# Squares of group B's outputs two steps later, and their roots one step later, in the lead to forgetting attention

## The reference, cut to what matters

```python
u = rmsnorm(h, g_attn)
qa, ka, va, logf, qb, kb, vb = project(u, w_in, b_forget)
oa = fox_prompt(qa, ka, va, logf)          # group A: forgetting attention, 8 heads x 64
ob = swa_prompt(qb, kb, vb, rel_bias, sinks)  # group B: sliding window, 8 heads x 64
mixed = jnp.concatenate([rmsnorm(oa, g_out_a), rmsnorm(ob, g_out_b)], axis=-1)
h = h + mixed @ w_out
u = rmsnorm(h, g_ffn)
return h + (jax.nn.silu(u @ w_gate) * (u @ w_up)) @ w_down
```

## Time and profile before

| | |
|---|---|
| three runs | 1477.64, 1479.68, 1480.71 us; median 1479.68 |
| profiled execution | 1480.0 us, its span 1478.1 us |
| TensorE busy | 1409.9 us (95% of the span) |
| VectorE, ScalarE, GpSimd busy | 579.4, 481.2, 213.1 us |
| mean granted TensorE clock | 0.980 |
| chain that ended last | TensorE 89%, VectorE 4%, issue 2%, ScalarE 2% |

### The profile page before, as it was taken

One profiled execution on the slowest core, in us unless ns is written; L12 is line 12 of the kernel. 1 busy time (PEld: TensorE's weight loads), 2 busy tenths in 40 slices (PEclk: granted clock), 3 DMA queues, 4 the chain that ended last, 5 costly groups with the idle time before them and its releaser, 6 DMA issues.

```text
span 1478.1 us, 22602 instructions
## 1 busy us (share of the span) xinstructions
PE 1409.9 (95%) x9041; PEld 1302.7 (88%) x9041; DVE 579.4 (39%) x1378; ACT 481.2 (33%) x1049; POOL 213.1 (14%) x317
## 2 busy tenths in 40 slices
PE   5989989899999899999999999999999999999996
PEld 3878878778888767788999999999999999999996
DVE  6235553423232342374324343333333342524155
ACT  6335553554545454264220212111111212121103
POOL 2125453253524232000000000000000000000000
PEclk9999999999999999999999999999999999999998
DMA  7611113311212154333211111111120202020003
GB/s 195 112 41 47 33 48 96 120 49 41 91 41 73 28 187 145 132 85 104 86 43 44 43 43 44 44 43 44 43 61 26 72 15 72 22 79 29 1 1 118
DMA packets 110255, 97.64 MB, mean 66 GB/s; under 512 B 15936, under 2 KB 96928, under 8 KB 109640
## 3 DMA queue, kind: packets, MB, share of 16 engines
q1 hardware_dynamic: 110152, 96.20, 22.2%
HBM read 77.07 MB, written 19.21 MB: 65 GB/s over the span
## 4 chain that ended last, share of the span: by engine, by line
PE 89%; DVE 4%; issue 2%; ACT 2%; DMA 1%; POOL 0%; SPq 0%; DVEq 0%; ACTq 0%
PE ps L576 28%; PE ps L577 26%; PE ps L578 26%; PE ps L780 3%; PE ps L922 1%; DVE ps L1589 1%; PE ps L710 1%; PE ps L792 1%; PE ps L748 1%; DMA out<-raw 1%; PE ps L657 1%; PE ps L590 1%; DVE sp_w L1601 1%; PE ps L853 0%; DVE raw L1862 0%
## 5 line engine op out<-in xcount | busy, mean ns | idle before, releaser
L1819 DVE TENSOR_TENSOR outs<-outs,ps 128x384 f32<-128x384 f32 (+1 forms) x264 | 134.6, 510 | 108.6 <-PE ps L578 108.6
L1971 POOL TENSOR_TENSOR pl_x<-sp_x,ph_x 128x512 fp32r<-128x512 f32 (+5 forms) x120 | 102.1, 863 | 180.2 <-ACT sp_x L1224 178.6
L1804 DVE TENSOR_TENSOR gu<-ps,sg 128x384 f32<-128x384 f32 (+1 forms) x66 | 34.6, 524 | 237.8 <-PE ps L578 237.8
L1403 ACT ACTIVATE h_hi<-gu 128x384 fp32r<-128x384 f32 (+1 forms) x66 | 32.9, 498 | 222.3 <-DVE gu L1804 222.3
L1223 ACT ACTIVATE ph_x<-ps,negc 128x512 fp32r<-128x512 f32 (+5 forms) x120 | 63.1, 525 | 87.9 <-PE ps L792 87.9
L1397 ACT ACTIVATE sg<-ps 128x384 f32<-128x384 f32 (+1 forms) x66 | 30.5, 465 | 171.7 <-PE ps L578 171.7
L576 PE MATMUL ps<-f_hi,ff0hi 128*128 128x384 f32 (+1 forms) x264 | 85.7, 325 | 0.0
L576 PE MATMUL ps<-f_hi,ff3hi 128*128 128x384 f32 (+1 forms) x264 | 85.6, 324 | 0.0
L576 PE MATMUL ps<-f_hi,ff2hi 128*128 128x384 f32 (+1 forms) x264 | 85.6, 324 | 0.0
L576 PE MATMUL ps<-f_hi,ff1hi 128*128 128x384 f32 (+1 forms) x264 | 85.6, 324 | 0.0
L577 PE MATMUL ps<-f_lo,ff0hi 128*128 128x384 f32 (+1 forms) x264 | 85.2, 323 | 0.0
(11 more groups left out here) (311 smaller groups left out, 3809.2 us busy)
## 6 DMA issues: line engine op xcount, KB each, us to landing
raw<-in_w_gate SPq DMA_DIRECT2D x22, 512.0 KB, 4.7
raw<-in_w_up SPq DMA_DIRECT2D x22, 512.0 KB, 4.7
raw<-in_w_down SPq DMA_DIRECT2D x22, 512.0 KB, 4.0
raw<-in_w_in SPq DMA_DIRECT2D x14, 512.0 KB, 4.1
cb<-c_scratch SPq DMA_DIRECT2D x4, 1312.0 KB, 7.0
xt<-in_x_prompt SPq DMA_DIRECT2D x8, 512.0 KB, 4.4
out<-outb SPq DMA_DIRECT2D x16, 256.0 KB, 2.5
ob<-o_scratch SPq DMA_DIRECT2D x16, 256.0 KB, 3.0
```

The lines of the kernel that those rows point to most:

```text
L1403: act.activation(h_hi[par][:, f, c0:c0 + n], gu[(f + c) % 2][:, 0:n], ACT.Copy).then_inc(S["g_hi"], 1)
L1804: dve.tensor_tensor(gu[(f + c) % 2][:, 0:n], bank(3 + c, n), sg[c][:, 0:n], ALU.mult)\
L1819: add = dve.tensor_tensor(y, y, bank(6 + o % 2, whole * P).rearrange("p (t m) -> p t m", t=whole), ALU.add)
L1971: pool.tensor_tensor(pl_x[at][0:rows, 0:n], sp_x[at][0:rows, 0:n], ph_x[at][0:rows, 0:n].bitcast(F32), ALU.subtract).then_inc(S["x_pl"], 1)
```

## The change

Two constants. `SQ_AT` says behind which steps v which tiles are squared, and `ROOT_AT` behind which step the roots are taken. Before, tiles 0 and 1 are squared in step -7, then two tiles a step, tile 8 in step -3, and the roots stand in step -2. Now tiles 0 and 1 are squared in step -5, tile 8 in step -1, and the roots stand in step -1, behind tile 8.

```diff
-SQ_AT = {v: tuple(range(2 * (v + 7), min(2 * (v + 7) + 2, TILES))) for v in range(-7, -2)}
-ROOT_AT = -2
+SQ_AT = {v: tuple(range(2 * (v + 5), min(2 * (v + 5) + 2, TILES))) for v in range(-5, 0)}
+ROOT_AT = -1
```

## The result

| | before | after |
|---|---|---|
| median of 10 runs each | 1478.38 us | 1484.41 us |
| lowest, highest | 1477.09, 1480.72 us | 1479.73, 1486.79 us |
| profiled execution, its span | 1480.0, 1478.1 us | 1483.33, 1481.4 us |
| mean granted clock in it | 0.980 | 0.978 |

The ratio of the times is 1.0035, with a 95% interval of 1.0024 to 1.0046: 5.2 us slower (3.5 to 6.8). The forecast was 4.1 us more than before.

The account below looks back on a forecast made before the run. TensorE bounds the kernel: its work, idle time and low clock. 1480.0 - 3.4 + 6.0 + 1.5 = 1484.1 us against the profiled execution, 1483.8 against the median; range 1479.6 to 1486.6.

Parts of the forecast that it names:

- First term: TensorE's first wait in the lead: without the squares, restart 1.95 us sooner and clock held, 1.45: 3.4 us sooner.
- rival (d): Removing the squares gives nothing, as the store lands later or another wait ends last: 1487.2 us, chance 0.06.
- rival (a): The clock falls behind the 2.3 us first wait too, so the gain is 1.95 alone: 1485.2 us, chance 0.17.
- Second term: Ahead of the exponentials: tile 8's load waits behind the weight, then square and roots follow; exponentials 6.0 us late.
- rival (b): Tile 8's load isn't held by the weight; exponentials 4.0 us late, clock costs about 1: 1481.3 us, chance 0.14.
- (c): Loads keep up with ScalarE; exponentials 2.8 us late, clock holds: 1479.1 us, chance 0.13 shared with a faster case.
- Third term: Clock falls behind TensorE's nearly 6 us of idle time at the scores: 1.5 us, bounded by 0 and 3.

Follow-up runs that it names:

- e1: Kernel before with squares 2 and 3 moved behind the third turn (step -5), square 8 and the roots in step -2: 1475.23 us, ratio 0.9975.
- e4: e1 with SyncE issuing the first turn's store ahead of the weight load in step -7: 1475.67 us, ratio 0.9980 to the kernel before.
- e2: Kernel after with the loads behind squares 6 and 7, tile 8's among them, issued ahead of the weight load in step -2: 1479.99 us, ratio 1.0001.
- e5: Kernel after with Copy in place of Sqrt in group B's two roots, so both table loads vanish: 1478.37 us, ratio 0.9996.
- e8: Kernel after with 32 throwaway matmuls, 24 behind step 0's projection and 8 ahead of step 1's scores: 1484.39 us, ratio 1.0042.
- e11: e3 with 12 throwaway matmuls of 384 columns ahead of step 1's scores: 1480.0 us, ratio 1.0008 to the kernel before.
- e3: Kernel before with the roots alone one step later (step -1), all squares where they were: 1479.68 us, ratio 1.0005.
- e6: e1 with the roots one step later (step -1): 1476.49 us, ratio 0.9989 to the kernel before.

## Why the prediction was right, point by point

**First term (3.4 us sooner): right, shown.** The restart came 2.43 us into idle time where 2.3 was forecast, held by the store of `outb` (0.86 us at 258.69) as argued, and the clock stayed at 1.00. The profile gives 3.36 us up to step 0's scores; `e1` alone is 3.7 us faster (2.1 to 5.3). The prediction has all of TensorE's later work come earlier by this much; alone, in `e1`, it is 2.5 us from step 1 on. That removes rival (d); rival (a) falls with the clock row of 262 to 265. `e4` shows the store as the holder.

**Second term (exponentials 6.0 us late): right, 0.35 short.** The two executions differ by 4.73 us by this point (1.37 from the start, 3.36 from the first term). With that added, the weight was issued at 279.26 (forecast 279.2), the square of tile 8 started at 283.60 (283.3) and the exponentials at 287.35 (287.0). `e2` shows the mechanism: with the load ahead of the weight the wait is gone, and the loss with it. So rival (b), that the weight doesn't hold the load, and (c), that loads keep up, are out. `e2` makes (c)'s condition true, and the exponentials are 2.76 us late where (c) has 2.8. Its ratio of 1.0001 also meets (c)'s 1479.1 us, but not by (c)'s account: (c) has the clock hold, and it fell, so that to step 2 `e2` is 2.1 us longer than before and not 0.6 shorter. The roots' 3.07 us is right as well: 3.01 us from 279.61 to 282.62, and `e5`, without table loads, says 2.45 us for these. By the Trainium skill, ScalarE: Activation LUTs, section What ACT_TABLE_LOAD costs, two switches would be 5.3 us; the trace doesn't agree, and decides. (The prediction sets these 5.3 us against 3.07 us, which hold three activations too; against the two loads' own 2.56 us the sum would be 2.7 us larger, not 2.2.) The fit that the prediction takes from the Trainium skill, DMA: Bandwidth & Descriptors, stands there in the section Anatomy of one DMA — SWDGE (gpsimd) path, for DMAs that GpSimd issues. For the weight, which SyncE issues, it would give 3.2 us as an estimate, and the trace has 3.9.

**A detail that was too brief.** The forecast had 5 to 6 us of idle at step 1's scores, released by the exponentials. Of the 6.07 us only the last 1.63 is released by them. The first 4.44 us ends with VectorE's minima, which stand behind the reciprocals and hold the last transpose. Since the exponentials end later in any case, the size is not touched.

**Third term (clock, 1.5 us): too small in place, and not found in the whole.** In step 1 it is 2.54 us (6.52 against 3.98), inside the bounds of 0 and 3. But `e8` and `e11` hold the clock there, take those 2.5 to 3 us back within the step, and end at the same time as without. In the whole, a term of its own for step 1's clock is not borne out. Where the time goes instead is not shown.

**Sum.** By the profile to step 2 the change costs -3.36 + 6.35 + 2.54 = 5.5 us (35.81 against 30.29), and the whole time 5.2 us (3.5 to 6.8); forecast was 4.1. That these agree is in part luck: `e2`, `e3`, `e5` and `e6` lost 1.9 to 4.5 us more up to step 2 than in the whole. Nor does the sum come out without the clock: -3.36 + 6.35 is 3.0 us, below the interval. Why the kernel after, whose clock fell at step 1 too, kept its whole loss is open. In its profile the two later stretches, 338 to 350 and 418 to 430, have a clock of 0.86, between `e3`'s 1.00 and the 0.72 of the kernel before.

## What to carry to other kernels

Moving work from one in-order queue's busy place to another is two changes: here the place left was worth 3.4 us, and the place entered made the exponentials 6.35 us late, 3.6 us of it because the last load was then issued behind a 512 KB one (`e2`). Take the first without the second (`e1`: only the items that plug), and put the small load that others wait for ahead of the big one that nobody needs yet (`e2`). Both in one kernel were not run. A stretch's loss in the profile is not the program's loss as long as the clock is part of it; the whole time of a control run decides.

## What of the hardware was not expected

A 64 KB load issued right behind a 512 KB one in the same queue took 3.9 us against 1.7 alone: issued 0.42 us behind the big one, which also took 3.9 us, it landed 0.4 us behind it. Idle time of 2.44 us ahead of the minima left the clock at 1.00 (`e1`), while 0.31 and 1.93 us on either side of three short transposes came with a fall to the 1.2 GHz level at step 1 (`e3`); the length of one wait alone doesn't tell. And in `e11` a fall avoided at one place was followed by falls at two others, some 55 and 135 us on, where `e3` has none; that this is cause is not shown. Holding the clock with throwaway work gained nothing that the whole time shows (`e11`, `e8`).
